# Retention columns of the last tile and the sample projected between expert slots; sample keys transposed in pairs

## What is computed

```python
hn = rms_norm(h, g_mix)
rq, rk, rv, rg, nq, ck, cv, sk, sv, wk, wv, ng = jnp.split(hn @ w_in, cuts, axis=-1)   # 4x512, 512, 6x128, 24
rq = rotary(ret_heads(rq), pos, HD_RET, RET_THETA)                  # the "retention columns" are rq, rk, rv, rg
rk = rotary(ret_heads(rk), pos, HD_RET, RET_THETA) * HD_RET ** -0.5
o_ret, s_new = retention(rq, rk, rv, s0)                            # chunk by chunk, carries a state; the sample has its own
h = h + mixer_output(o_ret, rg, gn_g, o_cmp, o_slc, o_win, gates, w_out)
h = h + mem_attend(rms_norm(h, g_mem), mk, mv, w_mq, w_mo)          # 4 heads over 256 memory tokens
h = h + peer_ffn(rms_norm(h, g_ffn), p_wq, p_keys, p_u, p_v)        # 8 heads x 16 experts chosen for each token
```

## Time and profile before

| | us |
|---|---|
| median of 3 runs | 2066.08 (2061.32 to 2073.36) |
| profiled execution | 2071.42 |
| its span, first to last instruction | 2069.6 |
| prologue, until the first gather of expert rows | 404.6 |
| slots and end | 1665.0 |

### The profile page before, as it was taken

How to read it: one execution, slowest core, us unless ns; L and a number is a source line. 1 busy time by engine, 2 the same in 40 slices (tenths; PEclk the granted TensorE clock), 3 DMA queues, 4 the chain that set the end, 5 groups by cost and what they waited for, 6 DMA issues and landing times.

```text
span 2069.6 us, 20390 instructions
## 1 busy us (share of the span) xinstructions
PE 1695.1 (82%) x6117; PEld 867.3 (42%) x6117; DVE 1334.7 (64%) x3133; ACT 959.6 (46%) x3115; POOL 679.7 (33%) x560
## 2 busy tenths in 40 slices
PE   8999999778877568887839779878598899889965
PEld 3533465534443324543516545444234343536221
DVE  1121032398878689977756799878676876665565
ACT  3000132255455355555536555555355654553445
POOL 0000000133435343433435433434347553333442
PEclk9999979878989888989979989988799999896898
DMA  6131636399999999999999998999999999998997
GB/s 205 41 123 41 204 127 228 128 380 359 379 417 418 330 388 382 346 417 418 416 386 378 420 352 340 411 418 409 396 339 367 415 416 414 418 414 324 376 419 302
DMA packets 134862, 696.50 MB, mean 337 GB/s; under 512 B 23288, under 2 KB 32856, under 8 KB 66464
## 3 DMA queue, kind: packets, MB, share of 16 engines
q0 software_dynamic: 78016, 562.07, 67.6%
q1 hardware_dynamic: 56736, 133.13, 17.6%
HBM read 683.91 MB, written 15.43 MB: 338 GB/s over the span
## 4 chain that ended last, share of the span: by engine, by line
PE 42%; DMA 28%; DVE 15%; issue 6%; ACT 5%; POOL 3%; SPq 1%; another core or an unknown queue 0%; ACTq 0%; DVEq 0%; POOLq 0%
DMA arena<-in_peer_uv,expert 23%; PE bank L1585 13%; PE bank L948 11%; DVE arena L2568 5%; DVE arena L2580 4%; PE bank L1157 4%; DMA arena<-in_cache_win_k 2%; POOL arena L894 2%; PE bank L1239 2%; PE bank L1275 1%; PE bank L1224 1%; PE bank L1362 1%; PE bank L1524 1%; PE bank L1024 1%; POOL arena L855 1%
## 5 line engine op out<-in xcount | busy, mean ns | idle before, releaser
L894 POOL DMA_INDIRECT arena<-in_peer_uv,expert x512 | 627.4, 1225 | 1344.8 <-DVE arena L2580 545.6
L1585 PE MATMUL bank<-arena 128*128 128x512 f32 (+1 forms) x1340 | 759.0, 698 | 269.0 <-ACT arena L2008 258.8
L2568 DVE CUSTOM_DVE_ANT_0 arena<-arena 128x1024 f32<-128x1024 f32 x520 | 635.4, 1222 | 317.7 <-DMA arena<-in_peer_uv,expert 310.0
L1585 PEld LDWEIGHTS bank<-arena 128*128 128x128 f32 (+1 forms) x1340 | 261.9, 214 | 590.7 <-ACT arena L2008 332.9
L1995 ACT ACTIVATE arena<-arena 128x1 f32<-128x1 f32 x520 | 104.1, 200 | 617.2 <-DVE arena L2568 616.2
L2580 DVE SCALAR_TENSOR_TENSOR arena<-arena 128x1024 f32<-128x1024 f32 x185 | 236.7, 1280 | 5.8 <-ACT arena L2000 5.8
L948 PE MATMUL bank<-arena 128*128 128x512 f32 (+3 forms) x560 | 228.8, 567 | 0.0
L2000 ACT ACTIVATE arena<-arena 128x1 f32<-128x1 f32 x520 | 201.2, 387 | 17.3
L1998 ACT ACTIVATE arena<-arena 128x1 f32<-128x1 f32 x520 | 193.8, 373 | 0.2
L948 PEld LDWEIGHTS bank<-arena 128*128 128x128 f32 (+1 forms) x560 | 93.7, 170 | 132.0 <-issue 126.9
L2008 ACT ACTIVATE arena<-arena 128x128 f32<-128x128 f32 (+1 forms) x335 | 134.3, 401 | 31.6 <-ACT arena L2000 1.1
(11 more groups left out here) (299 smaller groups left out, 1937.6 us busy)
## 6 DMA issues: line engine op xcount, KB each, us to landing
arena<-in_w_out SPq DMA_DIRECT2D x10, 2048.0 KB, 16.6
arena<-in_peer_wq SPq DMA_DIRECT2D x10, 2048.0 KB, 18.4
arena<-in_w_in SPq DMA_DIRECT2D x6, 2048.0 KB, 7.9
arena<-in_w_mq SPq DMA_DIRECT2D x5, 2048.0 KB, 28.0
arena<-in_w_mo SPq DMA_DIRECT2D x5, 2048.0 KB, 31.0
arena<-in_peer_uv,expert POOLq DMA_INDIRECT x512, 10.9
sc_proj<-arena SPq DMA_DIRECT2D x3, 1676.0 KB, 5.4
arena<-sc_proj SPq DMA_DIRECT2D x3, 1676.0 KB, 11.3
```

The source lines that it names most:

```text
L894: pool.indirect_dma_start(out=ring[:, p % RING, :], out_offset=None, in_=a["peer_uv"], in_offset=bass.IndirectOffsetOnAxis(ap=idx, axis=0) ...
L1585: ins = pe.matmul(banks[6 + half][0:R, :], diag[:, n % NDIAG, 0:R], ring[:, k, D + half * 512:D + (half + 1) * 512], start=(p == FIRST_PE[ ...
L2568: dve.tensor_tensor_reduce(out=ring[:, k, 0:D], in0=ring[:, k, 0:D], in1=x, scale=GELU_B, scalar=0.0, op0=ALU.mult, op1=ALU.add, accum_out ...
```

## The change

**Projection.** The eight units (chunk 0 to 3) x (tile 3, sample) leave the prologue (`B_UNITS`); 27 units stay (`A_UNITS`). The normalised, transposed rows of these tiles, 557 KB, are stored (`sc_hnT`), read back after front 1, and the units run in slots 94 to 126 (`REST_AT`), four slots for each. For that SyncE loads chunks 0 to 3 of `w_in` again, 2 MB each, into two buffers, chunk 2 and 3 only after the sample's unit of chunk 0 and 1 has been stored. ScalarE evicts into four staging buffers, VectorE rotates there, SyncE stores each piece to `sc_proj[3]` or `sc_heads` and waits for it to land before the next.

**Plan.** The three fronts become shorter (90 slots to 83: the prompt's attention starts three steps earlier and the memory attention is packed into 12 steps). New places: front 2 from slot 131, pages 213, front 3 257, the sample's attention 342. The sample's state step moves from slot 90 to 315, beside front 3, with buffers of its own, and its loads go in front 3's list of weights. In slots 384 to 487 VectorE takes three of eight rows instead of two.

**Sample keys.** A transpose takes 128 columns, two key groups at once; the scores are two matmuls on the two halves of the partitions, into two banks: 8 steps for the window, 16 for the pages.

The core of the diff:

```diff
+RET_CHUNKS = (0, 1, 2, 3)
+B_TILES = (3, PT)
+A_UNITS = [(c, t) for c in CHUNK_ORDER for t in range(NT) if c not in RET_CHUNKS or t not in B_TILES]
+B_UNITS = [(c, t) for c in RET_CHUNKS for t in B_TILES]
...
-    return t < PT and s % 8 in ((1, 4, 6) if t < PT - 1 else (2, 6))
+    return t < PT and s % 8 in ((1, 4, 6) if p < 488 else (2, 6))
...
-FRONT_AT = {0: 0, 1: 0, 2: 108, 3: 242}
-STATE_AT, PAGES_AT, SMIX_AT, SGRP_AT = 90, 198, 332, 414
-A_AT = 15
+FRONT_AT = {0: 0, 1: 0, 2: 131, 3: 257}
+REST_AT, STATE_AT, PAGES_AT, SMIX_AT, SGRP_AT = 94, 315, 213, 342, 414
+A_AT = 12
...
-        WK_AT = SMIX_AT + 8
-        KA_AT = WK_AT + 24
+        WK_AT = SMIX_AT + 14
+        KA_AT = WK_AT + 21
...
             sp.wait_ge(qp_done, 2 * H)
+            sp.dma_start(hnT_b, sc_hnT).then_inc(spilled, 16)
+            rest_weights(0)
+            rest_weights(1)
+            sp.wait_ge(spilled, 16 * (PT + 1))
+            for u, (chunk, t) in enumerate(B_UNITS):
+                sp.wait_ge(proj_ready, NA + u + 1)
+                if chunk in (0, 1):
+                    sp.wait_ge(rotated, B0 + u + 1)
+                src = stage[0:rows_of(t), u % 4, :]
+                dst = sc_proj[t][:, 512 * chunk:512 * chunk + 512] if t < PT else sc_heads[chunk]
+                sp.dma_start(dst, src).then_inc(spilled, 16)
+                if t == SAMPLE and chunk + 2 in RET_CHUNKS:
+                    rest_weights(chunk + 2)
+                sp.wait_ge(spilled, 16 * (PT + 2 + u))
             sp.dma_start(pj, sc_proj[2]).then_inc(proj_loaded, 16)
-            sp.wait_ge(s_ret_ready, 1)
-            sp.dma_start(sc_ret.rearrange("b (h d) -> (b h) d", d=HD), s_rows[0:64, S_Y, :]).then_inc(scratch_stored, 16)
-            sp.wait_ge(scratch_stored, 32)
             output_weights(2)
             group_weights(2)
...
+            def rest_of_projection():
+                for u, (chunk, t) in enumerate(B_UNITS):
+                    R, b = rows_of(t), 2 + u % 4
                     for k in range(KC):
+                        yield REST_AT + 4 * u + k // 2
+                        if k == 0:
+                            if u == 0:
+                                pe.wait_ge(spilled, 16 * (PT + 1))
+                            if t == B0:
+                                pe.wait_ge(w_in_loaded[chunk % 2], 16 * (4 + chunk // 2))
+                            bank = claim(b)
+                        w = half_w[chunk % 2].rearrange("p (k n) -> p k n", k=KC)
+                        ins = pe.matmul(bank[0:R, :], hnT_b[:, k, row_block(t)], w[:, k, :],
                                         start=(k == 0), stop=(k == KC - 1))
...
-                def page_transposes(gi, keys, row, cc):
+                def key_transposes(gi, pieces):
                     bank = claim(gi % 2)
-                    for q in range(4):
-                        j = 4 * cc + q
-                        ins = pe.transpose(bank[0:HD, q * P:(q + 1) * P], keys[:, row, j * HD:(j + 1) * HD], ident)
+                    for q, piece in enumerate(pieces):
+                        ins = pe.transpose(bank[:, q * P:(q + 1) * P], piece, ident)
...
+                def key_scores_of(bg, dst, keys):
+                    for x in range(2):
+                        half = slice(64 * x, 64 * x + 64)
+                        ins = pe.matmul(dst[x], q_mask[half, bg, :], keys[half], start=(bg == 0), stop=(bg == BG - 1))
+                    return ins
...
             def background():
                 yield from front(1, FRONT_AT[1])
-                yield from state_rows()
+                yield from rest_of_projection()
                 yield from front(2, FRONT_AT[2])
```

More of the change, by code:

```diff
@@ L45, with chunk_done, row_block @@
 BUF_OF = {5: 0, 4: 1, 0: 0, 1: 1, 2: 0, 3: 1}
-NCH = len(CHUNK_ORDER)
-def evicted(chunk, t):
-    return NT * CHUNK_ORDER.index(chunk) + t + 1
+RET_CHUNKS = (0, 1, 2, 3)
+B_TILES = (3, PT)
+B0 = B_TILES[0]
+A_UNITS = [(c, t) for c in CHUNK_ORDER for t in range(NT) if c not in RET_CHUNKS or t not in B_TILES]
+B_UNITS = [(c, t) for c in RET_CHUNKS for t in B_TILES]
+NA = len(A_UNITS)
+HB = P * (PT - B0) + DB
+def evicted(chunk, t):
+    return A_UNITS.index((chunk, t)) + 1
+def chunk_done(chunk):
+    return max(n for n, unit in enumerate(A_UNITS) if unit[0] == chunk) + 1
+def row_block(t):
+    return slice(P * (t - B0), P * (t - B0) + rows_of(t))
 RING = 7
@@ L260, in trunk_kernel @@
         tri = ar.take(P)
+        DECAY = ar.at - base.at
         decay = ar.take(H, P)
@@ L771, in _ @@
             output_weights(3)
             group_weights(3)
-            sp.wait_ge(state_ready, PT)
-            sp.dma_start(out["p_state"][0, 0].rearrange("h d e -> d h e"), state[0:HD, :, :]).then_inc(y_stored, 16)
+            state_out = out["s_state"][0].rearrange("b h (x d) e -> x (b h) d e", x=2)
+            sp.wait_ge(s_state_step, 2)
+            for x in range(2):
+                sp.dma_start(state_out[x], s_state[64 * x:64 * x + 64]).then_inc(s_stored, 16)
+            sp.wait_ge(s_ret_ready, 1)
@@ L1179, in memory_attention @@
             def memory_attention(gi, at):
-                grp = groups[gi]
-                for s in range(2 * HM + 5):
+                grp, v0 = groups[gi], HM * gi
+                for s in range(MEM_LAST):
                     yield at + s
-                    if s % 2 == 0 and s // 2 < HM:
-                        hh = s // 2
-                        v, b = HM * gi + hh, hh % 2
+                    if s - 4 in MEM_HEADS:
+                        hh = MEM_HEADS.index(s - 4)
+                        b = 5 - hh % 2
@@ L1384, in branch_rows @@
                     freed[3] = (s_nsa_ready, 1) if kind else (s_branch, 2)
-                for s in range(BG + 2):
+                for s in range(WIN_STEPS + 2):
                     yield WK_AT + s
@@ L1591, in expert_row @@
                         freed[6 + half] = (sum_added, 2 * t + 2)
-            steps, keys = background(), route_keys()
+            steps, keys, states = background(), route_keys(), state_rows()
             for p in range(NSLOT):
@@ L1660, in _ @@
                 copy_rowsT(hnT, t * P, rows_of(t))
-            for n in range(NT - 2, NCH * NT):
+            for n in range(NT - 2, NA):
                 evict(n)
@@ L1908, in branch_rows @@
                     act.activation(s_o[0:HD, 0, :], banks[5][0:HD, 0:64], ACT.Copy).then_inc(s_oT_ready, 1)
-                for s in range(1, BG + 1):
+                for s in range(1, WIN_STEPS + 1):
                     yield WK_AT + s
```

447 lines of the change are left out of this document (241 added, 206 removed).

## The result

The changed kernel takes 2094.74 us in the median of three runs (2079.14 to 2100.45), against 2066.08 us (2061.32 to 2073.36). The ratio is 1.016, with a 95% interval of 1.012 to 1.020: slower by 1.6%, where the forecast was 2.1% faster. The profiled execution took 2094.7 us, span 2092.9.

The account below looks back on a forecast made before the run. The prologue's projection was taken as bound by TensorE, the loop after the first gather by transfers at 418 GB/s. -55 + 3 + 24 - 10 - 12 - 5 + 11 = -44 us, from 2066.1 to 2022 us; range 1992 to 2052.

Parts of the forecast that it names:

- prediction's own sign of being wrong: Loop from first gather to end shrinks or grows by over 30 us, or time goes to a stretch not named.
- Units leave the prologue, -55 + 3: Prologue: eight units of 6.88 us TensorE time go, -55 us; loads coming late behind row stores and spill, +3.
- prologue rival: Prologue: SyncE's row stores make what follows late, 25 of the 55 us lost, 2047 us; first gather after 360; chance 0.03.
- Bytes, +24: Loop: 10.06 MB more to move, costing 24.1 us at 418 GB/s if the stretch is bound by transfers.
- State step, -10: State step moved beside front 3: wait for its small-row load goes, 14.8 us, less 5 for VectorE work there.
- The sample's attention, -12: Sample's attention: window keys asked for six slots earlier, removing 15 of TensorE's 18.8 us wait; 12 taken of 0 to 17.
- Last tile, -5: Stretch of the sample's memory values: two of twelve rows move from TensorE to VectorE, winning 3.4 to 7 us, taken 5.
- New waits, +11: Loop: TensorE waits for chunks 2 and 3 and tile 2's rows, 7 us, and for the page weights, 4 us.
- the 95 to 110: Slots 94 to 126, the moved units: expected time in us, at about 400 GB/s, as sign for bytes and new waits.
- rival of the denser plan: Loop: shorter fronts give half back through sample's attention, state step and waits, net -21 us, 2045 us; chance 0.24.
- chain through SyncE: Moved units: piece stores queue behind 2 MB chunks on SyncE, three turns lose 75 us, net +24, 2090 us; chance 0.08.
- speculation on tiles: Sample's key scores: two array halves run matmuls in parallel, halving 52.9 us; 5 us below the forecast, 2017; one in ten.

Follow-up runs that it names:

- e3: Changed kernel with SyncE's 22 prologue row stores issued ahead of the compression-weight load; ratio 1.012 to the kernel before, first gather at 353.1 us.
- e4: Changed kernel with both the later page gathers of e1 and the earlier row stores of e3; 0.994 of the kernel before, 2047.5 us.
- f1: e4 with the four 2 MB loads of projection weights between expert slots cut to their first eighth; 0.987 of the kernel before.
- f2: e4 with the state step's four long VectorE operations cut to 2 of their 32 planes; 0.996 of the kernel before.
- h1: f4 with the two loads of the state cut from 64 rows to 8 rows each; 0.985 of the kernel before.
- e1: Changed kernel with the four groups of page gathers of the sample's attention issued later in GpSimd's list; 0.997 of the kernel before.
- e2: Kernel before with its four groups of page gathers moved earlier, 2 to 3 slots behind the releasing TensorE step; 1.020 of the kernel before, 2095 us.
- g1: f4 with the seven loads of retention rows cut from 64 rows to 8, and the last state's store to one of 8 heads; 0.988 of the kernel before.
- f4: e4 with compression weights and window loads put in turn, values leaving once keys have landed; 0.991 of the kernel before, 2039.9 us.
- f3: e4 with the old spacing inside a front put back and fronts 2 and 3 begun 3 slots earlier; 1.002 of the kernel before.
- h2: f4 with the state loaded by eight transfers of 2 KB row pieces instead of two of 8 KB rows; 0.986 of the kernel before, 2038.3 us.

## Why the prediction was wrong, point by point

The prediction's own sign of being wrong came: from the first gather on the kernel took 68 us more, over the 30 that it named. Of these, 24 are the bytes that were forecast and 29 lie in the sample's attention.

1. *Units leave the prologue, -55 + 3.* 44.3 us measured. The eight units went as counted; the charge of 3 us for what is late next should have been 11. It was the prologue rival's mechanism at less than half of its price of 25 (the first gather at 360.3 us stands at the 360 that was to be its sign): with the stores first the gathers start 51.1 (e3) and 53.6 us earlier (e4), the forecast to 2 us.
2. *Bytes, +24.* Right: 650.0 MB against 639.8 from the first slot on are 24 us at 418 GB/s, and f1 has them cost it: there the stage of the units saved 14.6 us for 6.0 MB, 2.4 us a MB, which is the price of the rows at 418 GB/s. By the 358 GB/s that the Trainium skill gives ("DMA: Bandwidth & Descriptors", Specifications) it would be 2.8, an estimate from that figure; these rows do not bear it out.
3. *State step, -10.* Its old stretch lost its excess (15 us at slots 88 to 104, under 1 now). What I expected to come back was VectorE's 5 us; f2 shows no cost of it, while slots 296 to 320 took 10 us more above their bytes (8 in e4) than slots 281 to 305 of before, as far behind the start of front 3; h1 puts some 5 us of that on the load of the state. Together 4 us are won (6 in e4) for the 10 forecast, and the reason was wrong.
4. *The sample's attention, -12.* **The step that failed**: +29 us of excess, 41 us beside the forecast. I costed TensorE's list, ScalarE's copies and the window load, and did not look at what the compressed plan does to GpSimd's list, where page gathers with waits stand between expert gathers. e1 takes 35 us of slots 352 to 416 away with nothing but their places, and e2 adds 29 us to them in the kernel before. With that mended the stage has 13 to 22 us of excess against 19, so that no gain is left to be seen, since the other half of the step failed too. The window's wait stayed at 15.2 us (18.8 before) instead of going: the keys are asked for earlier, but take 55.2 us to land instead of 39. In both kernels the DMA engines were full from the issue to the landing (share 1.02 to 1.03, 395 to 408 GB/s), and the gathers beside the keys went on for 46 us of the 55 after the change, for 25 of the 39 before.

```profile
arena<-in_cache_win_k SPq DMA_DIRECT2D x1, 2048.0 KB, 55.2
```

5. *Last tile, -5.* The rest of the loop, slots 416 or 414 on, has 2.5 us less excess, less than it varies by between kernels. In the stretch that the point named, slots 464 to 479, no gain is seen: excess 12.4 us before and 13.6 after. The same slots went with 1.7 in e2 and none in g1, where TensorE's granted clock was 0.87 and 0.86 there; in the other kernels it was 0.64 to 0.73, with 7 to 14 us. This stretch makes most of what the rest varies by.
6. *New waits, +11.* TensorE waited 8.5 us for a chunk, once (I had said 6 to 10, twice), and 11.8 in two waits for reloaded rows, against 7.2 in one before; the units' slots 94 to 126 took 101 us, inside the 95 to 110. The pages cost 6 us for the 4 forecast, and f4 gets them back.
7. *Not in the sum.* Fronts 2 and 3 take as long as before up to their output projection, in three slots fewer, with 5 and 7 us more excess. The rival of the denser plan named this, but gave it no price: its three terms are the sample's attention, the state step and the waits. f3 shows that the old spacing does not cure it. Front 1 gave back 6 us unforeseen.

Put together for e4, by spans: -53.6 prologue, +24 bytes, +6 excess = -23.4 (2069.6 to 2046.2); the forecast had the excess fall by 16 (points 3 to 6). So the step in GpSimd's list, 38 us by e1, is the largest part of the miss and not all of it: with both repairs e4 is at 0.994, which is 2053 us on the 2066 of before and still just outside the range that ended at 2052. For the changed kernel: -44.4 + 24 + 43.5 = +23.

The rival "chain through SyncE" gave 2090 us, close to the result, and is not what happened: its place, slots 94 to 131, ran at 397 GB/s with 6 us of excess. That a rival's number comes out is no evidence for its mechanism.

The speculation on tiles is borne out: the halves of the key scores do run at once. Two matmuls of 64x512 (four records) in the changed kernel, and one (two records) in the kernel before, both at full clock:

```profile
1636.47 1.08 PE L1439 MATMUL bank<-arena 64*64 64x512 f32 x4
```
```profile
1652.54 1.07 PE L1362 MATMUL bank<-arena 64*64 64x512 f32 x2
```

The same time for twice the matmuls agrees with the Trainium skill ("TensorEngine Tiling (Array Packing)", Key Properties), that different tiles of the array run in parallel. In all the score matmuls were busy for 27.0 us instead of 52.9. That brought no time that the stage shows (13 to 22 us of excess with the gathers mended, 19 before).

## What to carry to other kernels

When a plan is compressed, look for every list that works in order and runs ahead: what matters to a wait in it is the distance to the step that ends it, in units of that engine's lead, and transfers queued behind the wait pay for it. Put such transfers as late as their use allows: here four to five slots too early cost 38 us, two to three cost 12 (17 of the 35 us in the stage). And in a loop bound by transfers, read each stage as time above its bytes: saved slots and saved instructions count only where this excess is.

The best kernels here that leave nothing out are f4 and h2 (page gathers late, row stores first, loads in turn; in h2 the state in pieces too), about 1.0% and 1.4% faster than before with intervals that overlap. The 4 us between their profiled executions lie in slots 464 to 479 (excess 12.3 and 7.0), which h2 does not touch.

## What the runs showed of the hardware

- While 1 MB of state is loaded in 8 KB rows beside the gathers (f4), the DMA engines are full at 249 to 301 GB/s instead of 418 for some 15 us; in pieces of 2 KB (h2) at 312 to 356; with an eighth of the load (h1) the dip is gone. Some 420 fewer packets under 512 bytes in that stretch changed nothing (348 and 347 GB/s).
- With GpSimd's waits TensorE's mean granted clock in slots 352 to 416 was 0.76, between its two levels (1.2 and 2.4 GHz, 0.5 and 1.0), and 0.83 with the waits gone; the same 794 matmul records were busy for 176.0 and 161.3 us. In the kernel before, putting the waits in (e2) took it from 0.93 to 0.85, and some 815 records from 178.1 to 190.5 us. So holes in the gathers make the matmuls of the stage slower, too.
- A load of 2 MB took 55.2 us with gathers issued beside it for 46 us, and 39 with gathers for 25 us, after which they had stopped for want of it: asking earlier did not make it come earlier by as much.
